# A two-layer diffusion backbone with grouped experts: weights laid out by partition on the host, modulation units summed in two groups, and a hint on PE's expert loop

## The reference

```python
sh1, sc1, g1, sh2, sc2, g2 = split(silu(c) @ ada_w[l] + ada_b[l], 6)    # ctx: the same with c_ctx
h = rms(x, attn_norm_g[l]) * (1 + sc1) + sh1
x = x + g1 * (attention(h @ w_in[l]) @ w_out[l])    # 8 global, 8 local heads; latents also attend to ctx
h = rms(x, ffn_norm_g[l]) * (1 + sc2) + sh2
# router: best of 4 groups, 2 of its 4 experts per token
x = x + g2 * sum_e(gate_e * ((silu(h @ w_gate[l, e]) * (h @ w_up[l, e])) @ w_down[l, e]))
```

## Time and profile before

| | us |
|---|---|
| median of 3 runs | 1176.32 (1174.71 to 1176.94) |
| the profiled execution | 1175.42 |
| its span | 1173.7 |
| PE busy | 999.1 (85%) |
| DVE busy | 464.6 (40%) |
| ACT busy | 345.3 (29%) |
| start to first projection | 0 to 48 |
| layer 0: q/k/v and attention | 48 to 293 |
| layer 0: projection, norm, routing | 293 to 386 |
| layer 0: experts, gathering of rows | 386 to 736 |
| layer 1: q/k/v to routing | 736 to 923 |
| layer 1: experts, output | 923 to 1174 |

### The profile page before, as it was taken

The page is one execution under the profiler, slowest core; times in us unless marked ns, Lnnn a source line. Parts: engine busy times, 40 slices in busy tenths (PEclk is TensorE's granted clock), DMA queues, the critical chain, the costliest instruction groups (busy, mean ns, idle before and its releaser), DMA issues.

```text
span 1173.7 us, 27007 instructions
## 1 busy us (share of the span) xinstructions
PE 999.1 (85%) x11017; PEld 630.7 (54%) x11018; DVE 464.6 (40%) x1248; ACT 345.3 (29%) x806; POOL 35.1 (3%) x65
## 2 busy tenths in 40 slices
PE   5699998888997799999999965898988884756897
PEld 2244644533436467676666644586667552433554
DVE  1356666566225322222222215586833531322343
ACT  3312255655014122222222223325732210111121
POOL 0000000000000000000000002000000000000000
PEclk9899999999995999999999986899998997887899
DMA  8993099798403079896989978106033299999981
GB/s 310 402 375 125 18 362 355 272 320 306 178 24 120 6 265 388 304 393 245 349 330 353 345 290 315 43 1 233 2 144 144 104 394 395 394 393 393 395 322 36
DMA packets 122416, 297.53 MB, mean 253 GB/s; under 512 B 4944, under 2 KB 6240, under 8 KB 122368
## 3 DMA queue, kind: packets, MB, share of 16 engines
q1 hardware_dynamic: 116672, 285.49, 65.4%
q0 software_dynamic: 3984, 11.15, 2.9%
q10 hardware_dynamic: 1712, 0.23, 0.1%
HBM read 288.85 MB, written 15.86 MB: 260 GB/s over the span
## 4 chain that ended last, share of the span: by engine, by line
PE 72%; DMA 7%; DVE 7%; SPq 6%; ACT 3%; issue 3%; ACTq 1%; POOL 0%; DVEq 0%; POOLq 0%
PE bank L624 18%; PE bank L441 10%; PE bank L636 9%; PE bank L612 8%; PE bank L541 7%; SPq L296 5%; DMA ring<-in_w_up_dram 4%; PE bank L511 3%; PE bank L384 3%; PE bank L482 3%; PE bank L494 2%; DMA ring<-in_ada_w_dram 2%; PE bank L665 2%; PE bank L575 2%; PE bank L450 1%
## 5 line engine op out<-in xcount | busy, mean ns | idle before, releaser
L624 PE MATMUL bank<-ring,h_t 128*32 128x256 f32 x4160 | 252.7, 397 | 67.4 <-DMA ring<-in_w_up_dram 50.0
L624 PEld LDWEIGHTS bank<-ring,h_t 128*32 128x32 f32 x4160 | 158.3, 115 | 155.0 <-issue 94.0
L1254 DVE TENSOR_TENSOR h_t<-h_t,bank 128x128 f32<-128x128 f32 x65 | 18.7, 288 | 276.4 <-ACT h_t L882 276.4
L636 PE MATMUL bank<-ring,h_t 128*32 128x256 f32 x2080 | 126.3, 381 | 2.1 <-ACT h_t L889 2.1
L441 PE MATMUL bank<-h_t,ring 128*128 128x512 f32 (+1 forms) x320 | 117.0, 520 | 12.3 <-ACT h_t L790 12.3
L612 PE MATMUL bank<-tokm,h_t 128*32 128x256 f32 x1760 | 110.8, 385 | 8.5 <-DVE h_t L1228 8.5
L889 ACT COPY h_t<-bank 32x256 f32 x168 | 61.3, 365 | 150.9 <-PE bank L636 92.8
L882 ACT ACTIVATE h_t<-bank 128x128 f32<-128x128 f32 x65 | 18.1, 278 | 295.8 <-PE bank L624 295.8
L636 PEld LDWEIGHTS bank<-ring,h_t 128*32 128x32 f32 x2080 | 73.7, 110 | 42.3 <-issue 10.2
L441 PEld LDWEIGHTS bank<-h_t,ring 128*128 128x128 f32 x320 | 62.1, 195 | 59.9 <-issue 40.5
L612 PEld LDWEIGHTS bank<-tokm,h_t 128*32 128x32 f32 x1760 | 67.3, 111 | 37.7 <-issue 10.2
(11 more groups left out here) (164 smaller groups left out, 1035.7 us busy)
## 6 DMA issues: line engine op xcount, KB each, us to landing
ring<-in_w_gate_dram SPq DMA_DIRECT2D x32, 2048.0 KB, 12.7
ring<-in_w_up_dram SPq DMA_DIRECT2D x32, 2048.0 KB, 16.6
ring<-in_w_down_dram SPq DMA_DIRECT2D x32, 2048.0 KB, 15.4
ring<-in_ada_w_dram SPq DMA_DIRECT2D x24, 2048.0 KB, 11.2
ring<-in_w_in_dram SPq DMA_DIRECT2D x8, 1536.0 KB, 16.7
y_rows<-in_table_dram SPq DMA_DIRECT2D x1, 8704.0 KB, 44.1
ring<-in_w_out_dram SPq DMA_DIRECT2D x4, 2048.0 KB, 10.2
y_rows<-h_t POOLq DMA_DIRECT2D x42, 128.0 KB, 5.4
```

What stands on the lines that cost most here:

```text
L624: last = mm(o.rearrange("r (s c i) -> r s c i", s=2, c=KF), hc_t[:, k, :], w[:, :, k, :, CHUNK * q:CHUNK * q + CHUNK], start=(k == 0), sto ...
L636: last = mm(bank[4][CHUNK * q:CHUNK * q + CHUNK, 0:256], he_t[:, k, :], wd[:, k, 256 * q:256 * q + 256], start=(k == 0), stop=(k == KF - 1))
```

## The change

**Host layout.** `by_partition` rearranges the six weight tensors on the host so that what one load brings to a partition is one contiguous piece: 16 KB (12 KB for `w_in`). The bytes on chip end up where they were.

**Modulation in two groups.** `ADA_GROUPS` keeps units 0 to 3 alone and joins 4 to 11 and 12 to 23. In a group, unit u uses a window of 32 columns of `scv_wide` (62 columns per row block, zero but for the two of `scv` in the columns 30 and 31), so that its two rows of results land in rows 2(u-u0) of each column group, and all units of the group accumulate in bank 7. Copy, transposes and sum are done once per group, at n = 22 or 58 (ScalarE), 24 or 60 (PE) and 25 or 61 (VectorE). The sum is four reduces over q.

**Hint.** PE's loop over experts is made with a hint at the top of the body that names its closing branch.

```diff
+ADA_GROUPS = [(0, 1), (1, 2), (2, 3), (3, 4), (4, 12), (12, 24)]
...
+def by_partition(name, a):
+    import numpy as np
+    if name == "ada_w":
+        a = a.reshape(DEPTH, KD, P, 12, 512).transpose(0, 3, 2, 1, 4).reshape(DEPTH, 12, P, KD * 512)
+    elif name == "w_in":
+        a = a.reshape(DEPTH, 4, 2, P, IN_W).transpose(0, 1, 3, 2, 4).reshape(DEPTH, 4, P, 2 * IN_W)
+    elif name == "w_out":
+        a = a.reshape(DEPTH, 2, 4, P, D).transpose(0, 1, 3, 2, 4).reshape(DEPTH, 2, P, 4 * D)
+    elif name in ("w_gate", "w_up"):
+        a = a.reshape(DEPTH, NE, KD, P, FE).transpose(0, 1, 3, 2, 4).reshape(DEPTH, NE, P, KD * FE)
+    elif name == "w_down":
+        a = a.reshape(DEPTH, NE, KF, P, D).transpose(0, 1, 3, 2, 4).reshape(DEPTH, NE, P, KF * D)
+    return np.ascontiguousarray(a)
...
+        scv_wide = h_t[:, 6, 0:496].rearrange("p (k c) -> p k c", k=KD)
...
             def load_ada(s, u, signal):
                 l, m = divmod(u, 12)
-                sp.dma_start(slot(s, KD), ada_w[l, :, m * 512:m * 512 + 512].rearrange("(k p) n -> p k n", p=P)
-                             ).then_inc(signal, 16)
+                sp.dma_start(ring[:, s, :], ada_w[l, m]).then_inc(signal, 16)
...
-                    s, w, k = expert_weights(e, a)[part]
-                    src = w[l, bass.ds(e, 1)].rearrange("a (k p) n -> p (a k) n", p=P)
-                    sp.dma_start(slot(s, k), src).then_inc(ew_in[l][s], 16)
+                    s, w = expert_weights(a)[part]
+                    src = w[l, bass.ds(e, 1)].rearrange("a p n -> p (a n)")
+                    sp.dma_start(ring[:, s, :], src).then_inc(ew_in[l][s], 16)
...
-                if u > 3:
-                    pe.wait_ge(ada_summed, u)
-                elif u > 0:
-                    pe.wait_ge(parts_ready, u)
+                n = [u0 <= u < u1 for u0, u1 in ADA_GROUPS].index(True)
+                u0, u1 = ADA_GROUPS[n]
+                if u == u0 and n > 3:
+                    pe.wait_ge(ada_summed, n)
+                    pe.wait_ge(scv_spaced, 1)
+                elif u == u0 and n > 0:
+                    pe.wait_ge(parts_ready, n)
                 w = ring[:, s, :].rearrange("p (k n) -> p k n", k=KD)
                 for k in range(KD):
                     q = k % 4
-                    last = mm(bank[7][32 * q:32 * q + 2, :], scv[:, k, :], w[:, k, :],
-                              start=(k < 4), stop=(k >= 4))
+                    if u < 4:
+                        last = mm(bank[7][32 * q:32 * q + 2, :], scv[:, k, :], w[:, k, :],
+                                  start=(k < 4), stop=(k >= 4))
+                    else:
+                        first_col = 30 - 2 * (u - u0)
+                        last = mm(bank[7][32 * q:32 * q + 32, :], scv_wide[:, k, first_col:first_col + 32], w[:, k, :],
+                                  start=(u == u0 and k < 4), stop=(u == u1 - 1 and k >= 4))
                 last.then_inc(ada_used, 1)
...
-            def ada_turn(u):
-                pe.wait_ge(parts_ready, u + 1)
-                if 0 < u < 4:
-                    pe.wait_ge(ada_summed, u)
+            def ada_turn(n):
+                pe.wait_ge(parts_ready, n + 1)
+                if 0 < n < 4:
+                    pe.wait_ge(ada_summed, n)
                 for m in range(4):
-                    last = turn(ada_bank(u)[:, P * m:P * m + P], parts[:, P * m:P * m + P], ident)
+                    last = turn(ada_bank(n)[:, P * m:P * m + P], parts[:, P * m:P * m + P], ident)
                 last.then_inc(ada_turned, 1)
...
-                        if l == 0 and i % 3 == 0 and 0 < i <= 60:
-                            ada_turn(3 + i // 3)
+                        if l == 0 and i in (24, 60):
+                            ada_turn(4 if i == 24 else 5)
...
-                with pe.Fori(0, 5) as i:
+                with nc.Fori(0, 5, engines=[pe.engine], hint_back_edge=True) as i:
...
-            def ada_parts(u):
-                act.wait_ge(ada_used, u + 1)
-                if u > 0:
-                    act.wait_ge(ada_turned, u)
+            def ada_parts(n):
+                act.wait_ge(ada_used, ADA_GROUPS[n][1])
+                if n > 0:
+                    act.wait_ge(ada_turned, n)
                 do(parts, bank[7][:, :], ACT.Identity).then_inc(parts_ready, 1)
...
-                    if l == 0 and n % 3 == 1 and n // 3 < 20:
-                        ada_parts(4 + n // 3)
+                    if l == 0 and n in (22, 58):
+                        ada_parts(4 if n == 22 else 5)
...
-            def ada_sum(u):
-                dve.wait_ge(ada_turned, u + 1)
-                ps = ada_bank(u)[:, :].rearrange("p (m q x) -> p m x q", m=4, q=4)[:, :, 0:2, :]
-                v.tensor_reduce(mods[:, 4 * u:4 * u + 4, :], ps, AX.X, ALU.add).then_inc(ada_summed, 1)
+            def ada_sum(n):
+                dve.wait_ge(ada_turned, n + 1)
+                u0, u1 = ADA_GROUPS[n]
+                ps = ada_bank(n)[:, :].rearrange("p (m q j x) -> p m j x q", m=4, q=4, x=2)
+                sums = mods[:, 4 * u0:4 * u1, :].rearrange("p (j m) x -> p m j x", m=4)
+                for m in range(4):
+                    last = v.tensor_reduce(sums[:, m], ps[:, m, 0:u1 - u0], AX.X, ALU.add)
+                last.then_inc(ada_summed, 1)
             def add_bias(m0, m1):
-                dve.wait_ge(ada_summed, m1 // 4)
+                dve.wait_ge(ada_summed, 4 if m1 == 2 * KD else len(ADA_GROUPS))
...
+                if l == 0:
+                    link(v.memset(scv_wide, 0.0))
+                    v.tensor_copy(scv_wide[:, :, 30:32], scv[:, :, :]).then_inc(scv_spaced, 1)
...
-                    if l == 0 and n % 3 == 0 and 0 < n <= 60:
-                        ada_sum(3 + n // 3)
+                    if l == 0 and n in (25, 61):
+                        ada_sum(4 if n == 25 else 5)
```

More of the change, by code:

```diff
@@ L238, in backbone, with ada_bank @@
         yq_ready, scattered = sem("yq_ready"), sem("scattered")
+        scv_spaced = sem("scv_spaced")
         dve_step = sem("dve_step")
-        def ada_bank(u):
-            return bank[2 if u < 4 else 7]
+        def ada_bank(n):
+            return bank[2 if n < 4 else 7]
         def units(l):
@@ L252, in keys, with expert_weights @@
             return (0, 512) if tt < 2 else (256, 256)
-        def expert_weights(e, a):
-            return [(3 * a, w_gate, KD), (3 * a + 1, w_up, KD), (3 * a + 2, w_down, KF)]
+        def expert_weights(a):
+            return [(3 * a, w_gate), (3 * a + 1, w_up), (3 * a + 2, w_down)]
         def first_of(engine, l, e):
@@ L273, in _ @@
         def _(sp):
-            def slot(s, k):
-                return ring[:, s, :].rearrange("p (k n) -> p k n", k=k)
             def load_ada(s, u, signal):
                 l, m = divmod(u, 12)
-                sp.dma_start(slot(s, KD), ada_w[l, :, m * 512:m * 512 + 512].rearrange("(k p) n -> p k n", p=P)
-                             ).then_inc(signal, 16)
+                sp.dma_start(ring[:, s, :], ada_w[l, m]).then_inc(signal, 16)
             def load_win(l):
                 for q in range(4):
-                    sp.dma_start(win[:, 2 * q:2 * q + 2, :],
-                                 w_in[l, 256 * q:256 * q + 256, :].rearrange("(k p) n -> p k n", p=P)
+                    sp.dma_start(win[:, 2 * q:2 * q + 2, :].rearrange("p k n -> p (k n)"), w_in[l, q]
                                  ).then_inc(win_in[q], 16)
             def load_wout(l, half):
-                sp.dma_start(wout[half], w_out[l, 512 * half:512 * half + 512, :].rearrange("(k p) n -> p k n", p=P)
-                             ).then_inc(wout_in[half], 16)
+                sp.dma_start(wout[half].rearrange("p k n -> p (k n)"), w_out[l, half]).then_inc(wout_in[half], 16)
             def load_expert(l, e, a, parts=(0, 1, 2)):
                 for part in parts:
-                    s, w, k = expert_weights(e, a)[part]
-                    src = w[l, bass.ds(e, 1)].rearrange("a (k p) n -> p (a k) n", p=P)
-                    sp.dma_start(slot(s, k), src).then_inc(ew_in[l][s], 16)
+                    s, w = expert_weights(a)[part]
+                    src = w[l, bass.ds(e, 1)].rearrange("a p n -> p (a n)")
+                    sp.dma_start(ring[:, s, :], src).then_inc(ew_in[l][s], 16)
             def refill(l, e, a):
@@ L1378 @@
     for name in _INS:
-        a = _np.ascontiguousarray(inputs[name])
+        a = by_partition(name, _np.asarray(inputs[name]))
         arrays[f"in_{name}_dram"] = a
```

## The result

| | us | ratio to before, 95% interval |
|---|---|---|
| before (its runs beside the changed kernel) | 1176.63 (1174.71 to 1177.57) | 1 |
| after, median of 4 runs | 1157.21 (1155.21 to 1159.05) | 0.9837 [0.9812, 0.9862] |
| after, the profiled execution | 1155.21 | |
| its span | 1153.5 | |

The changed kernel is faster by 19 us, where 27 were forecast: inside the range, and 8 us short. Between the profiled executions the span falls by 20.2 us. What is missing to the forecast lies in attention and, quite unforeseen, in the last microseconds of the program.

The account below looks back on a forecast made before the run. Bounds: the `ada_w` DMA at the start, TensorE in layer 0's attention, weight DMA in layer 1's experts. Layout -11.3, start -1.6, attention -14 and hint -0.2 sum to -27.1: 1149 us, range 1139 to 1163.

Parts of the forecast that it names:

- -11.3: Layer 1's expert weight refill: larger pieces move at 425 GB/s instead of 394, saving 11.3 us up to the thirteenth expert.
- The line through 2 and 6 KB: DMA rate for 16 KB pieces, extrapolated from 2 and 6 KB rows: 436 GB/s, the refill's bound of -15 us.
- that through 2 and 4 KB: DMA rate for 16 KB pieces, extrapolated from 2 and 4 KB rows: 412 GB/s, the refill's bound of -6.8 us.
- The start: Program start: first four `ada_w` blocks land 2.0 us sooner, four reduces add 0.4, net -1.6 us.
- the DMA doesn't cut 16 KB pieces to 4 KB: Layout rival on weight loads: DMA cuts the 16 KB pieces again, total only -17 us (1159 us); chance 0.1.
- pieces 16 KB apart cost no rate that shows: Slower rival on weight loads: reads 16 KB apart load memory unevenly; at 330 GB/s, +20 us (1196 us); chance 0.07.
- The 4 given back: Layer 0's attention: new waits of values matmuls for ScalarE's copy, 0.25 us each, 16 of them, 4 us.
- the softmax rival: Layer 0's attention: the softmax chain takes PE's place, -8.1 and +1.1 us there, total -20 (1156 us); chance 0.15.
- A new wait: ... PE stands some 1.3 us once: Layer 0's attention: unit 12 waits for its group's sum on VectorE behind maxima(25) and scale_probs(24), costing 1.3 us once.
- -18.9 + 4: Layer 0's attention: 18.9 us saved by removing 18 of 20 modulation rounds, less 4 us of new values waits.
- A hint can't save a fetch that isn't made: PE's expert loops: the body stays in the engine, so the hint is worth only -0.2 us; bounds -3.3 and +5.5.
- the rival that I gave 0.06: Hint rival at PE's back edges: the hint fetches a block again each time, PE waits, +5.5 us (total -21, 1155).

Follow-up runs that it names:

- run 8: Changed kernel without hint, loops at slot 64: unit 12 one PE iteration later, 1150.39 us; or first group's sum one softmax unit earlier, 1151.50 us.
- run 2: Only the hint added to the kernel before: 1180.72 us, ratio 1.0028.
- run 1: The changed kernel again, 1160.62 us (0.9855), and the changed kernel with only the hint taken out, 1201.48 us (1.0191).
- run 5: Changed kernel without the hint, both PE expert loops placed at slot 64: 1153.71 us (0.9812), again 1156.29 us (0.9808).
- run 6: Changed kernel with the hint, both PE expert loops placed at slot 64: 1155.28 us, ratio 0.9817.
- run 4: Kernel before with only layer 0's expert loop placed at slot 180, 1177.22 us (1.0008), or at slot 200, 1209.67 us (1.0279).
- run 7: Kernel before with the two modulation groups alone, its loops held at slots 128 and 86: 1169.75 us, ratio 0.9931.

## Why the prediction was right or wrong

**Where 20.2 us of span went**, by the same points of both traces: -0.9 at the first scores (146.26); -10.4 in attention; +0.5 up to layer 0's experts; +1.2 over these; -1.5 to the start of layer 1's; -12.8 to the thirteenth expert; -0.2 to the last `down`; +3.9 in the final scatter.

**Layout: right.** -12.8 for the refill against -11.3. At 428 GB/s, not 425, the same sum gives -12.3. The line through 2 and 6 KB (436) and that through 2 and 4 KB (412) did bracket it. The start gave -1.4 of -1.6. Stores of `y_rows` landed in 6.1 us (median; at most 7.0; the earlier trace rows has 5.4 and 6.2), well within 13. Two rivals fell: the DMA doesn't cut 16 KB pieces to 4 KB (28719 packets, and 428 is not 401), and pieces 16 KB apart cost no rate that shows (428). The rule of the Trainium skill that I weighed ("DMA: Bandwidth & Descriptors", section "Why small descriptors are slow (HBM only)"), from which 4% on gate and up follow, doesn't account for the gain: 428 against 387 at 2 KB is 11%.

**Attention: mechanism right, one term mis-sized.** By PE's groups the parts are: waits before L394 and L384 -12.2 (all of them, not 18 of 20), 72 transposes at 0.44 us for four -7.9, together -20.1 where 18.9 were forecast; waits before the transposes of probabilities and the values 3.5 + 1.1 = 4.6, where 4 were forecast; the stand 2.5; modulation matmuls +2.0 and values matmuls +0.7. That makes -10.3 of the -10.4. The 4 given back were right in size, but not in place: the prediction put them all before the values, where 1.1 came; 3.5 came before the transposes, where PE waits for VectorE's scaling, the sign that it had named for the softmax rival. That the sum fits is luck in part. The wrong step is "A new wait: ... PE stands some 1.3 us once". It was 2.5 us, and behind it the clock fell (1.5 us), which no term covered; run 8 gives 4.2 us for both, nearly 3 more than the term and most of the 3.6 that attention fell short. That VectorE had two maxima and two scalings in front of the sum could have been counted from the order of its loop. The softmax rival (-8.1 and +1.1) showed its sign but not its price: in run 8, with unit 12 out of the way, attention is 14.9 us shorter than before, which is the forecast's -18.9 + 4.

**The hint: wrong, by a step that looked safe.** "A hint can't save a fetch that isn't made" is true of the kernel before, as run 2 shows (it costs 3.3 us there). But the earlier trace rows describe the code at its old place, and part 2 of the same change moved the loop by 162 instructions, onto a place where the fetches are made. The move had no term in the sum at all. In the changed kernel the hint saves 41 us (run 1) and costs about 5 against a good place (run 5), of which 3.9 are the pause in the scatter and what the clock loses behind it, and 0.6 back edges. By itself, where neither a fetch nor a block's end is in its way, no cost of the hint is shown (run 6). My sum had -0.2 and a bound of +5.5; the net effect of hint and move on the time lay near that bound, so the rival that I gave 0.06 is nearest to what happened, though not by its mechanism: the block isn't fetched again at each edge, it is the block behind the loop that comes late. Without the hint this change would have been slower by 1.9%, a case that the list of rivals lacked. So it is luck that the time still lies in the range: the part that was costed at -0.2 took up 41 us that nobody had looked for.

**What the runs show of the mechanism, and what they don't.** Shown: the place of a body of 1601 instructions decides, 1781 slots from a block's start are well and 1801 are not; the hint takes the refetching away. My reading of it, argued and not shown: PE holds 8 blocks; without a hint the block behind the loop is fetched too, so that 7 of the body and one more fit and 8 and one more don't; the hint replaces that fetch by the back edge's target, so 8 fit, and the block behind the loop comes late. The last pass at slot 200, which fetched nothing again (run 4), doesn't follow from this reading. The late block was seen at both exits, each time where a block ends just behind the loop (runs 1 and 2). The size of 8 blocks itself was not varied. The Trainium skill ("Runtime: NRT & Kernel Launch", section "Instruction fetch mechanics") gives TensorE room for 2048 instructions in blocks of 256, which fits. It also says that a taken branch to outside the current two pages forces a fetch before execution goes on; the trace of before contradicts that for PE, with one block fetched in 270 us that hold four back edges over seven blocks.

**Additivity.** Layout -12.5, groups -8.1, hint +3.3 by themselves make -17.3 us; the whole change made -17.1 in the session of the first and the third. That agreement is good to the 3 us of the intervals, and it hides the 41 us: it holds only because the hint was there to take up what the groups' move of the code would have cost.

## What to carry to other kernels

Where a loop's body comes near to what its engine keeps of the code (here 7 blocks were kept and 8 weren't), count its instructions and find the slot at which it begins, before and after every edit ahead of it, also one that has nothing to do with the loop; the instruction queue's blocks in a later pass tell which side it is on, and a fixed slot settles it better than a hint. When units are joined into groups, the one wait that stays at the seam must be costed by counting the other engine's order in front of it, and a stand of 2.5 us on TensorE can cost its clock too (in six traces of seven here): move the unit that waits by one iteration. For pieces beyond the sizes in a trace, a constant plus a term in 1/size through rows of the same trace was good to 4%.

## What was not expected of the hardware

- Twenty instruction slots decide over 32 us (1177.2 at slot 180, 1209.7 at slot 200), with 27 blocks of 16 KB fetched more.
- A missing block costs PE 1.0 us (run 2) or 2.6 us (the changed kernel) when it is in the middle of running code, and 6.8 to 7.4 plus 2.4 to 2.7 (or 7.9 to 8.8 plus 0.9) at a back edge of a loop that is fetched again.
- After a stand of 2.5 us TensorE ran at half clock in six traces (16 matmuls in 3.39 to 3.56 us) and at full clock in a seventh (1.92 us, run 7); after one of 0.89 us at the same place the clock stayed up (1.92 us).
- 16 KB pieces moved at 428 GB/s with a DMA share of 1.01; 2 and 4 KB pieces, mixed, at 394.
